# Hybrid decoder layer on eight cores: rotary multiply-adds no longer put off, the last feature group of w_down in two halves of the tokens

## What is computed

```python
h = rmsnorm(x, g_pre_mix) * (1.0 + sc_a) + sh_a
fq, fk, fv, fg, sq, sk, sv = split(h @ w_in)
fox = forgetting_attention(fq, fk, fv, log_sigmoid(fg + b))   # 8 heads of 128, causal, decay from fg
sq = rope(sq, pos); sk = rope(sk, pos)                        # 8 query heads, 2 key heads
swa = sliding_window_sink_attention(sq, sk, sv, sinks)        # window 128
x = x + gt_a * rmsnorm(concat(fox, swa) @ w_out, g_post_mix)
h = rmsnorm(x, g_pre_mlp) * (1.0 + sc_m) + sh_m
y = square(relu(h @ w_up)) @ w_down                           # inner width 8192
x = x + gt_m * rmsnorm(y, g_post_mlp)
```

## Time and profile before

| | us |
|---|---|
| median of 3 runs | 3099.23 |
| lowest, highest | 3097.49, 3100.45 |
| the profiled execution | 3100.45 |
| its span, slowest core (5) | 3098.5 |
| spans of the eight cores | 3086.4 to 3098.5 |

### The profile page before, as it was taken

How to read it: one execution, slowest core, us unless ns; L and a number is a source line. 1 busy time by engine, 2 the same in 40 slices (tenths; PEclk the granted TensorE clock), 3 DMA queues, 4 the chain that set the end, 5 groups by cost and what they waited for, 6 DMA issues and landing times.

```text
span 3098.5 us, 38921 instructions; the slowest of 8 cores (3086.4 to 3098.5 us)
## 1 busy us (share of the span) xinstructions
PE 2898.8 (94%) x15016; PEld 1371.8 (44%) x15016; DVE 929.4 (30%) x1489; ACT 750.9 (24%) x1224; POOL 469.1 (15%) x614
## 2 busy tenths in 40 slices
PE   2799999999998899999999999999999999999993
PEld 1336543565444444444444444444444444444441
DVE  1323455345555357641111000000233211000005
ACT  1312344554555345431111000000111111000000
POOL 1000100000001256520000111111000000111114
PEclk9899999999999999999999999999999999999997
DMA  9755655444548223454444455555788544444455
GB/s 185 214 88 112 103 92 92 72 72 72 92 72 143 69 109 123 143 116 75 76 76 80 87 90 97 99 97 94 167 189 185 92 77 75 76 77 79 75 102 197
DMA packets 99782, 327.92 MB, mean 106 GB/s; under 512 B 12144, under 2 KB 12272, under 8 KB 93200
## 3 DMA queue, kind: packets, MB, share of 16 engines
q0 software_dynamic: 58896, 213.97, 42.1%
q1 hardware_dynamic: 40704, 111.46, 10.6%
HBM read 497.32 MB, written 42.01 MB: 174 GB/s over the span
## 4 chain that ended last, share of the span: by engine, by line
PE 84%; DVE 5%; DMA 4%; ACT 3%; issue 3%; POOL 1%; SPq 0%; DVEq 0%; POOLq 0%; ACTq 0%
PE bank L387 84%; POOL acc L407 1%; DVE bank L407 1%; DMA xstA<-xP 1%; DMA xstB<-xP 1%; DMA rmod<-wMA 1%; ACT Pb L404 1%; DVE mixF L412 1%; DVE bank L412 1%; ACT rr L404 1%; DMA rsh<-wMB 0%; ACT sq L404 0%; ACT acc L404 0%; DVE sq L412 0%; DVE Y L407 0%
## 5 line engine op out<-in xcount | busy, mean ns | idle before, releaser
L387 PE MATMUL bank<-mix,rung 128*128 128x512 bf16 x4096 | 884.9, 379 | 0.0
L387 PE MATMUL bank<-a,rung 128*128 128x512 bf16 x4096 | 884.4, 379 | 0.0
L387 PEld LDWEIGHTS bank<-mix,rung 128*128 128x128 bf16 x4096 | 400.8, 98 | 484.3 <-issue 1.7
L387 PEld LDWEIGHTS bank<-a,rung 128*128 128x128 bf16 x4096 | 400.8, 98 | 483.3
L387 PE MATMUL bank<-hT,ring 128*128 128x512 bf16 x1536 | 404.0, 388 | 3.0 <-DVE sq L412 1.5
L418 DVE TENSOR_SCALAR bank<-bank 128x512 f32<-128x512 f32 x256 | 166.1, 695 | 637.6 <-PE bank L387 637.6
L404 ACT ACTIVATE a<-bank 128x512 bf16<-128x512 f32 x256 | 153.1, 598 | 693.1 <-DVE bank L418 693.1
L421 DVE COPY mixF<-bank 128x512 f32<-128x512 f32 x64 | 41.2, 686 | 842.8 <-PE bank L387 842.8
L404 ACT ACTIVATE Pb<-bank,Ctok 128x512 bf16<-128x512 f32 (+1 forms) x320 | 194.3, 626 | 292.1 <-DVE bank L407 289.6
L407 POOL TENSOR_TENSOR acc<-acc,sq 128x512 f32<-128x512 f32 x180 | 225.3, 1266 | 220.7 <-ACT sq L404 216.1
L387 PE MATMUL bank<-mix,WO 128*128 128x512 bf16 x1024 | 235.8, 384 | 13.8 <-ACT sq L404 12.5
(11 more groups left out here) (129 smaller groups left out, 1614.1 us busy)
## 6 DMA issues: line engine op xcount, KB each, us to landing
rung<-wU POOLq DMA_DIRECT2D x128, 512.0 KB, 5.3
rung<-wD POOLq DMA_DIRECT2D x128, 512.0 KB, 5.3
ring<-wMB POOLq DMA_DIRECT2D x64, 512.0 KB, 6.1
ring<-wA POOLq DMA_DIRECT2D x38, 512.0 KB, 6.3
Y<-xP SPq DMA_DIRECT2D x16, 1024.0 KB, 4.9
x1s<-Y SPq DMA_DIRECT2D x16, 1024.0 KB, 3.9
outP<-mixF SPq DMA_DIRECT2D x64, 256.0 KB, 3.0
rmod<-wMA POOLq DMA_DIRECT2D x16, 512.0 KB, 26.4
```

Source lines behind the costliest of these rows:

```text
L387: ins = e.matmul(o, lhsT=l, rhs=rh, start=st, stop=sp)
```

## The change

Three things are changed.

1. `F.late` and what empties it are gone. The three rotary instructions enter DVE's queue at once behind ACT's half-copies.
2. In the second pass the groups 0 to 14 are done one by one, and group 15 in two halves: 64 matmuls for half 0 with all four weight tiles held, then 64 for half 1. The residual is loaded over the half-0 side of the `a` tiles (`aH`: each 128 x 512 float32 tile takes 1 KB in each of two neighbouring `a` tiles), as each weight tile's half-0 matmuls are done. The scaling and stores of half 0 (`finish(0, ...)`) are issued in the program behind the first weight tile of half 1, ahead of the evacuation of half 1.
3. `y_out` multiplies by the column `Av` in the second pass. The reciprocal root is copied to SBUF for POOL. Of 16 tiles of a half, POOL does five wholly (`m % 3 == 2`: two SBUF instructions), DVE eleven: a product into bank 4 or 5, then bank plus residual.

```diff
 class Fill:
-        def _late(self, n):
-            while self.late and self.late[0][0] <= n:
-                self.late.pop(0)[1]()
 def ev_rope(i, dstf):
                 act(rot(p=(0, 64)), bk(p=(64, 128)), AF.Copy)
                 act(rot(p=(64, 128)), bk(p=(0, 64)), AF.Copy)
-                def rest():
-                    stt(cs(), bk(), bs(slice(i, i + 1)), cosT(sl), ALU.add, ALU.mult)
-                    stt(rot(), rot(), bsw(slice(i, i + 1)), sinT(sl), ALU.add, ALU.mult)
-                    tt(dstf(sl), cs(), rot(), ALU.add)
-                F.late.append((F.n + 2, rest))
+                stt(cs(), bk(), bs(slice(i, i + 1)), cosT(sl), ALU.add, ALU.mult)
+                stt(rot(), rot(), bsw(slice(i, i + 1)), sinT(sl), ALU.add, ALU.mult)
+                tt(dstf(sl), cs(), rot(), ALU.add)
 def y_out(Tt, m, hf, bk):
-        cp(y, bk())
+        if Tt == 0:
+            cp(y, bk())
+        else:
+            ts(y, bk(), Av(3, slice(m, m + 1)), ALU.mult)
-    down(1, 2)
-    for i, (m, hf) in enumerate(todo):
-        dma("sp", aX(i), dram(T["x1s"][2 + hf][:, m, :], "x1s", 2 + hf, m // 4), f"gx{i % 16}")
-    fsb[0] = rstd_of(accs[0])
+    down(1, range(KC - 1))
+    bks = [next_ob(), next_ob()]
+    last = [R2.acq(("D", KC - 1, q)) for q in range(4)]
+    for q in range(4):
+        d_mms(bks, R2.bufs[last[q]], q, (0,))
+    y_out(1, KC - 1, 0, bks[0])
+    def xa(m, hf):
+        h = B["aH"].h
+        i = 32 * hf + 2 * m
+        cells = aT[i](slice(0, TS)).cells + aT[i + 1](slice(0, TS)).cells
+        return Acc(h[:, i:i + 2, 0, :], cells)
+    for hf in range(2):
+        for m in range(KC):
+            dma("sp", xa(m, hf), dram(T["x1s"][2 + hf][:, m, :].rearrange("p (a b) -> p a b", a=2), "x1s", 2 + hf, m // 4),
+                f"gx{(16 * hf + m) % 16}")
+    def finish(hf, ms, bk, rs):
+        for m in ms:
+            y = yp(1, m, hf)
+            x = xa(m, hf)
+            y2 = y.re(y.ap.rearrange("p (a b) -> p a b", a=2))
+            if m % 3 == 2:
+                tt(y, y, rs(), ALU.mult, eng="pool")
+                tt(y2, y2, x, ALU.add, eng="pool")
+            else:
+                t = banks[(4, 5)[m % 2]]
+                tt(t(), y, bk(), ALU.mult)
+                tv = t().re(t.h[:, :].rearrange("p (a b) -> p a b", a=2))
+                tt(y2, tv, x, ALU.add)
+            fin.append(dma("sp", dram(T["outP"][2 + hf][:, m, :]), y, f"go{(16 * hf + m) % 16}"))
+    for q in range(4):
+        d_mms(bks, R2.bufs[last[q]], q, (1,))
+        if q == 0:
+            fsb[0] = rstd_of(accs[0])
+            cp(sqb[0](), fsb[0]())
+            finish(0, range(KC), fsb[0], sqb[0])
+    y_out(1, KC - 1, 1, bks[1])
     fsb[1] = rstd_of(accs[1])
-    for i, (m, hf) in enumerate(todo):
-        y = yp(1, m, hf)
-        stt(y, y, Av(3, slice(m, m + 1)), fsb[hf](), ALU.mult, ALU.mult)
-        tt(y, y, aX(i), ALU.add, eng="pool" if i % 3 else "dve")
-        fin.append(dma("sp", dram(T["outP"][2 + hf][:, m, :]), y, f"go{i % 16}"))
+    cp(sqb[1](), fsb[1]())
+    finish(1, range(KC), fsb[1], sqb[1])
```

More of the change, by code:

```diff
@@ L376, in program @@
     aT = [B[f"a{i}"] for i in range(64)]
-    aX = B["aX"]
     def mm(out, lhsT, rhs, start, stop):
@@ L582, in col @@
     def col(out, slot_bufs, lhs):
-        F._late(1 << 30)
-        F._late(1 << 30)
         bk = out or next_pj()
@@ L691, in __init__ @@
             self.pend = []
-            self.late = []
             self.credit = 0.0
-        def _late(self, n):
-            while self.late and self.late[0][0] <= n:
-                self.late.pop(0)[1]()
         def _one(self):
-            self._late(self.n)
             while self.main:
@@ L734, in drain @@
                 self._one()
-            self._late(1 << 30)
             self.credit = 0.0
@@ L1301, in y_out, with d_mms, down @@
             dma("sp", dram(T["ys"][hf][:, m, :], "ys", hf, m), y, f"ys{i}")
[L1303 to L1306, removed]
-            for q in range(4):
[L1308 to L1321, removed]
+    def d_mms(bks, b, q, hfs):
+        mms = []
+        for i in range(16):
+            fc = 16 * q + i
+            for hf in hfs:
+                mms.append(mm(bks[hf](), b(slice(i * 128, i * 128 + 128)), aT[fc](slice(hf * TS, hf * TS + TS)), fc == 0, fc == 63))
+        pe(mms, [b()] + [aT[16 * q + i](slice(hf * TS, hf * TS + TS)) for i in range(16) for hf in hfs], [bks[hf]() for hf in hfs])
+    def down(Tt, ms):
+        for m in ms:
+            bks = [next_ob(), next_ob()]
+            for q in range(4):
+                s = R2.acq(("D", m, q))
+                d_mms(bks, R2.bufs[s], q, (0, 1))
+                R2.rel(s)
+            for hf in range(2):
+                y_out(Tt, m, hf, bks[hf])
     def per0(fc):
@@ L1329, in program @@
     assert not njobs
-    down(0, 0)
+    down(0, range(KC))
     fin = []
@@ L1364, in program @@
     assert state["c"] == 32
-    down(1, 2)
-    for i, (m, hf) in enumerate(todo):
-        dma("sp", aX(i), dram(T["x1s"][2 + hf][:, m, :], "x1s", 2 + hf, m // 4), f"gx{i % 16}")
-    fsb[0] = rstd_of(accs[0])
-    fsb[1] = rstd_of(accs[1])
-    for i, (m, hf) in enumerate(todo):
-        y = yp(1, m, hf)
-        stt(y, y, Av(3, slice(m, m + 1)), fsb[hf](), ALU.mult, ALU.mult)
-        tt(y, y, aX(i), ALU.add, eng="pool" if i % 3 else "dve")
-        fin.append(dma("sp", dram(T["outP"][2 + hf][:, m, :]), y, f"go{i % 16}"))
+    down(1, range(KC - 1))
+    bks = [next_ob(), next_ob()]
+    last = [R2.acq(("D", KC - 1, q)) for q in range(4)]
[7 more added lines that the diff above has]
+        return Acc(h[:, i:i + 2, 0, :], cells)
+    for hf in range(2):
+        for m in range(KC):
+            dma("sp", xa(m, hf), dram(T["x1s"][2 + hf][:, m, :].rearrange("p (a b) -> p a b", a=2), "x1s", 2 + hf, m // 4),
+                f"gx{(16 * hf + m) % 16}")
+    def finish(hf, ms, bk, rs):
+        for m in ms:
+            y = yp(1, m, hf)
[17 more added lines that the diff above has]
+    y_out(1, KC - 1, 1, bks[1])
+    fsb[1] = rstd_of(accs[1])
+    cp(sqb[1](), fsb[1]())
+    finish(1, range(KC), fsb[1], sqb[1])
     P.op("sp", None, extra=[d for d in fin])
@@ L1479, in build @@
         buf(f"a{i}", H + 2048 * i, [1024], BF16)
-    buf("aX", H, [32, TS], F32)
+    buf("aH", H, [64, 2, 256], F32)
     o = max(o, end1)
```

## The result

The changed kernel takes 3110.9 us (median; 3109.84 to 3112.16), the kernel before 3098.45: a ratio of 1.004, interval 1.002 to 1.0059. It is slower, by 12 us where 10 were forecast. Times and ratios here leave out executions in which the clock of half the chip was disturbed; the only profile of the halves alone is of such an execution and is read on core 7, in the other half. The profiled execution took 3109.84 us.

What follows compares the result with a forecast made beforehand. Bounds: TensorE waiting on the ScalarE-DVE rotary ping-pong, and DVE with POOL in the tail. Profiled 3100.45 + 25.5 - 15.5 = 3110.5, less 1.2 to the median: 3109 us; forecast 3102 to 3117 (chance 0.68), range 3097 to 3119.

Steps and rivals of the forecast that it cites:

- Part 1: Rotary stretch: attention subtracts move behind the rotary instructions on DVE, so TensorE waits longer; 25.5 us slower.
- about 40 us: Sign, 275 to 560 us: TensorE's waits for `bs`, a rotary multiply-add and `modT` sum to this instead of 18.
- The upper bound of 33: Rotary stretch: the most its cost was expected to be, in us; bounds from 3 to 33, taken 25.5.
- the loop: Rotary stretch: half-copies, rotary instructions, subtract, exponential, next copies on ScalarE and DVE; 4.22 + 0.70 k us for k subtracts.
- a slower TensorE hides in it, so I take 4: Rotary stretch: clock loss after longer waits, 8.5 us at most, partly hidden where the ScalarE chain sets the pace; 4 taken.
- Part 2: Tail after w_down: last group in halves and new DVE/POOL scaling; 15.5 us gained.
- My own chain: Tail: DVE's steps for both halves laid one after another, end 47.1 us after T0 against 64.7 before; gain 17.6.
- the bound of 13.4: Tail: gain in us if every DVE instruction had to wait for the one before, 4.2 less than 17.6.
- T0: Tail: the end of the first half of w_down's last group; span's end laid 64.7 us after it before the change.
- (a): Rival, rotary stretch: the ping-pong's lateness is absorbed, only about 4 us cost; 3088 us, chance 0.10.
- (b): Rival, rotary stretch: about half the cost, 12 us, if stripes begin with more slack; 3096 us, chance 0.14.
- (c): Rival, tail: gain only 5 us, as DVE and POOL block each other or loads come late; 3119 us, chance 0.08.

Runs made afterwards that it cites:

- the halves alone: Kernel before with w_down's last group done by halves and the residual loaded over `a`, final scaling and rotary as before: 3090.1 us, ratio 0.997.
- rotary alone: Kernel before with one edit, the three rotary instructions entering DVE's queue at once, tail as before: 3126.6 us against 3097.1, ratio 1.0095.
- tail alone: New kernel with `F.late` put back, rotary work put off by two steps again: 3081.67 and 3085.9 us; second run 3082.5, ratio 0.995.
- The run with banks in turn: Kernel with new tail, list not emptied, half 1's evacuations behind 9 final tiles; DVE's products now alternate banks 4 and 5: 3058.1 us against 3057.9.
- the kernel with one step of delay: New kernel with the rotary multiply-adds put off by one filler step instead of none: 3098.8 us, ratio 1.0005 to the kernel before.

## Why the prediction was right

**What bounds.** Right. PE's waits for DVE in the rotary stretch and DVE with POOL in the tail are where the time moved, and behind the output projection nothing else did: from the first output projection to the end go 2100.3 us before and 2100.7 with the rotary alone, 2084.8 in the new kernel and 2084.1 with the tail alone.

**Part 1: the mechanism right, the sum near by luck, its terms not.** I took 25.5 us, 21.5 of waits and 4 of clock. Up to the last `bs`, to which 18.5 of the waits were laid, PE's idle time grew by 14.6 us and its busy time by 11.0, 25.5 in all; up to the output projection it is 27.6, and by the times 28.4 (new kernel against the tail alone) to 29.5 (rotary alone). The waits that I said should sum to about 40 us made 32.7. Waits laid too long and a clock term taken too small cancel in part. The upper bound of 33 doesn't follow from the terms either: 21.5 + 8.5 are 30.

The laying held where the loop alone counts: the stripe of the earlier trace rows took 19.4 us from its first copies to `bs` (366.98 to 386.35), laid 19.55. `modT` came as laid: the wait became 3.4, 3.0 more. The failed step is "a slower TensorE hides in it, so I take 4": the clock took 11.0. The step holds in a stripe bound by ScalarE, not in the one with `modT`, where two waits follow each other. Windows of 2 us there:

```profile
422.00:424.00 2.00, 1.64 (x8) 0.68 (x9) 0.66 (x4) 0.00 (x0) 0.34 (x1) 0.50 0.01 4
424.00:426.00 2.00, 2.00 (x7) 0.76 (x5) 0.43 (x1) 0.69 (x1) 0.18 (x1) 0.50 0.58 66
426.00:428.00 2.00, 2.00 (x6) 0.71 (x5) 0.00 (x0) 0.00 (x0) 0.00 (x0) 0.50 0.97 195
428.00:430.00 2.00, 2.00 (x13) 1.01 (x12) 0.00 (x0) 0.00 (x0) 0.00 (x0) 0.96 0.02 2
...
442.00:444.00 2.00, 2.00 (x8) 0.39 (x7) 0.00 (x0) 0.78 (x3) 0.00 (x0) 0.50 0.35 123
```

After the wait of 3.39 us for `modT` (to 422.36) the clock stood at 1.2 GHz for three windows, some 2.8 us of work lost in 5.6 busy ones, where I had 1.7 for a wait, and ScalarE and DVE had nothing to do from 426 to 430: they waited for PE. After the next wait (2.92 us, to 441.3) it fell again. From `bs` to `bs` this stripe takes 31.3 us against 22.9 before: 8.4 more where I laid 4.1 of waits. The four stripes behind it grew by 4.1, 0.8, 1.7 and 0.6, laid 3.3, 0.3, 2.8 and 0.7; the three ahead of it by 0.7, 3.2 and 2.2, laid 0.95, 2.8 and 0.7; the start by 3.8, laid 2.8.

**Part 2: 15.4 against 15.5.** The chain is right; that the figure fits so well is luck. My own chain gave 17.6, and I took a value between it and the bound of 13.4. The chain was 2.2 us too short: 1.0 for each half's tiles and 0.6 between the halves, less 0.4 at the start (scaling began at T0 + 6.3, laid 6.7). DVE's tiles cost 1.49 us, not 1.40 (11 in 16.4 us, 3065.29 to 3081.67), because I took every product as free of the addition before it; with every third tile on POOL, two of DVE's in a row share a bank. The run with banks in turn shows that. The statistics matmul after the idle time took 2.04 us and not 1.02, 1.0 more where I took 0.4. The residual loads cost nothing in the time: 32 issues in 24.9 us from 3048.63, each landed after 5.4 to 9.2 us, and no final tile of DVE's waited.

I had priced them from one fast window, 396 GB/s in the earlier trace rows, so 21 us for all 32. That was wrong for the kernel before itself: its loads ran from 3006.3 to some 3043 us, 36 us, and the new ones, in pieces of 1 KB, took at most 33 (3048.6 to 3081.8). Before and then after, windows of the loads:

```profile
3020.00:3035.00 15.00, 15.00 (x71) 6.82 (x70) 0.00 (x0) 0.00 (x0) 0.53 (x1) 1.00 1.01 289
```
```profile
3056.00:3064.00 8.00, 8.00 (x37) 3.63 (x36) 0.75 (x1) 1.18 (x2) 1.26 (x1) 1.00 0.98 294
```

With the DMA engines as busy, both move some 290 GB/s; in windows of 4 us at a share of 0.9 or more both swing widely, 185 to 405 before and 161 to 383 now. Over the loads as a whole, their queue moved 8.39 MB in 63.6% of 40 us before (3006 to 3046) and 6.55 MB in 86.4% of 25 us now (3048 to 3073): an estimated 1.09 times the price per byte. The Trainium skill, DMA: Bandwidth & Descriptors, "Why small descriptors are slow", gave an estimated 4%. The trace is of that order and far from double the price; closer it can't tell, as other transfers share the engines in both windows.

**Rivals.** (a) falls: the lateness is not absorbed, and the 23.1 us for `bs` show it. (b), 3096, falls too: no half of part 1's cost was missing. It is the kernel with one step of delay that lands near there (3098.8). (c) falls with 0.69 us in all 44 instructions of DVE; its price of 1.7 us is real, but for the old scaling only.

## What to carry to other kernels

Where two in-order engines hand work back and forth, an instruction's place in its row can cost more than its length: put what a third engine waits for, however short, ahead of long work that nobody waits for yet. Look for a list that is emptied at a boundary; here that alone was worth 18 us, some 7 of them busy time that the clock gave back. When an engine's work at the end has been shortened, look at the transfers next: with DVE busy without a gap the end already lay 3 us further behind it than in the new kernel. And price a transfer from all of its windows: the fastest one told 21 us where the loads took 36.

## What the runs showed of the hardware

- DVE's add of 128x512 float32: 0.69 us with a bank as one operand, beside POOL or not; with both in SBUF 0.69 alone and 1.76 to 1.77 when it meets POOL's.
- The float32 statistics matmul (two of 128x512): 1.02 us behind other matmuls, 2.04 after 11 us of idle PE at a granted clock of 0.50.
- Waits of PE of 2.9 and 3.4 us were followed by one and three windows of 2 us at 0.50. With no wait over 1.5 us, the granted clock was 1.00 in each of the nine windows of 22 to 30 us from 335 to 560 us.
- On DVE, an instruction that reads the bank which the one before wrote, or writes the bank which it read, starts 0.79 to 0.80 us behind it; an independent one 0.61.
- The same matmuls of the rotary stretch (1332 in the trace, 1330 in the first case) kept PE busy for 210.5 us with 4.4 us of idle time, and for 227.5 us with 31.0.
- Loads in pieces of 2 KB at a DMA share of 1.01 to 1.04: 289 GB/s over 15 us, 396 over 8 us. In pieces of 1 KB at 0.98: 294. Per byte, an estimated 1.09 times the price over all of them.
